# Down projection with the activations as the stationary operand, and the sampled tokens in plain single precision on four column groups

## The reference

```
x = x + concat([oa, ob]) @ w_out
h = rms_norm(x, norm_ffn)                               # (288, 2048)
y = x + (silu(h @ w_gate) * (h @ w_up)) @ w_down        # w_gate, w_up: 2048 x 5632, w_down: 5632 x 2048
```

## Time and profile before

| | us |
|---|---|
| median of 3 runs | 1440.21 (1435.78 to 1446.68) |
| the profiled execution, its own time | 1442.6 |
| its span, first to last instruction | 1440.8 |
| PE busy | 1423.8 (99%) |
| DVE busy | 760.1 (53%) |
| ACT busy | 539.8 (37%) |

### The profile page before, as it was taken

One profiled execution on the slowest core, in us unless ns is written; L12 is line 12 of the kernel. 1 busy time (PEld: TensorE's weight loads), 2 busy tenths in 40 slices (PEclk: granted clock), 3 DMA queues, 4 the chain that ended last, 5 costly groups with the idle time before them and its releaser, 6 DMA issues.

```text
span 1440.8 us, 23855 instructions
## 1 busy us (share of the span) xinstructions
PE 1423.8 (99%) x10403; PEld 1375.2 (95%) x10403; DVE 760.1 (53%) x937; ACT 539.8 (37%) x650; POOL 116.0 (8%) x134
## 2 busy tenths in 40 slices
PE   6999999999999999999999999999999999999998
PEld 4999999998989899999999999999999999999998
DVE  4435655565543465744555464555555554545454
ACT  7336975321113433433233333333332333333322
POOL 2010421111220006100000000000000000000000
PEclk9999999997789999999999999999999999999999
DMA  8695555524455454655656556555555565655552
GB/s 235 176 324 136 160 142 148 135 73 115 117 155 187 133 163 147 169 155 174 172 151 176 154 168 173 161 165 173 150 176 158 164 172 152 174 166 162 170 168 74
DMA packets 320193, 231.32 MB, mean 161 GB/s; under 512 B 4838, under 2 KB 291823, under 8 KB 319514
## 3 DMA queue, kind: packets, MB, share of 16 engines
q1 hardware_dynamic: 314000, 206.06, 49.7%
q0 software_dynamic: 5856, 23.59, 5.4%
q10 hardware_dynamic: 234, 0.16, 0.0%
HBM read 219.99 MB, written 14.97 MB: 163 GB/s over the span
## 4 chain that ended last, share of the span: by engine, by line
PE 98%; DMA 1%; ACT 0%; DVE 0%; issue 0%; SPq 0%; ACTq 0%; DVEq 0%
PE acc L1450 29%; PE acc L1454 29%; PE acc L1451 28%; PE mx L1615 3%; PE mx L1687 1%; PE mx L1675 1%; PE mx L1405 1%; DMA reg_qkf<-in_x_prompt_dram 1%; PE acc L1470 1%; PE acc L1464 1%; PE mx L1544 0%; PE mx L1516 0%; PE mx L1476 0%; PE mx L1896 0%; PE mx L1590 0%; PE mx L1531 0%
## 5 line engine op out<-in xcount | busy, mean ns | idle before, releaser
L1450 PE MATMUL acc<-act_h,wh 128*128 128x288 f32 x2208 | 605.4, 303 | 0.0
L1451 PE MATMUL acc<-act_l,wh 128*128 128x288 f32 x2208 | 601.7, 298 | 0.0
L962 DVE TENSOR_TENSOR wl<-raw,wh 128x2048 fp32r<-128x2048 f32 x192 | 440.6, 2295 | 57.4 <-PE acc L1454 52.4
L609 ACT ACTIVATE wh<-raw 128x2048 fp32r<-128x2048 f32 x192 | 366.5, 1910 | 237.0 <-PE acc L1454 227.9
L1450 PEld LDWEIGHTS acc<-act_h,wh 128*128 128x128 f32 x2208 | 422.9, 192 | 5.1 <-issue 4.3
L1451 PEld LDWEIGHTS acc<-act_l,wh 128*128 128x128 f32 x2208 | 421.4, 191 | 0.0
L1454 PE MATMUL acc<-act_h,wl 128*128 128x288 f32 x2208 | 327.0, 301 | 0.0
L1454 PEld LDWEIGHTS acc<-act_h,wl 128*128 128x128 f32 x2208 | 306.3, 192 | 4.9 <-issue 4.7
L1450 PE MATMUL acc<-mix_h,wh 128*128 128x288 f32 x832 | 228.6, 299 | 0.0
L1451 PE MATMUL acc<-mix_l,wh 128*128 128x288 f32 x832 | 227.8, 295 | 0.0
L1450 PEld LDWEIGHTS acc<-mix_h,wh 128*128 128x128 f32 x832 | 157.1, 189 | 2.4 <-issue 2.3
(11 more groups left out here) (251 smaller groups left out, 765.4 us busy)
## 6 DMA issues: line engine op xcount, KB each, us to landing
raw<-in_w_in_dram SPq DMA_DIRECT2D x44, 1024.0 KB, 5.9
raw<-in_w_gate_dram SPq DMA_DIRECT2D x44, 1024.0 KB, 5.6
raw<-in_w_up_dram SPq DMA_DIRECT2D x44, 1024.0 KB, 5.6
raw<-in_w_down_dram SPq DMA_DIRECT2D x44, 1024.0 KB, 5.1
raw<-in_w_out_dram SPq DMA_DIRECT2D x16, 1024.0 KB, 5.4
reg_x<-in_state_hgrn_dram POOLq DMA_DIRECT2D x8, 512.0 KB, 5.0
out_dram<-reg_x POOLq DMA_DIRECT2D x8, 512.0 KB, 4.4
bias_rows<-bias_line POOLq DMA_DIRECT2D x1, 3072.0 KB, 15.4
```

Source lines behind the costliest of these rows:

```text
L609: nc.scalar.activation(wh[:, s % WH, :], raw[:, s % RAW, :], ACT.Copy).then_inc(high_done, 1)
L962: nc.vector.tensor_tensor(wl[:, s % WL, :], raw[:, s % RAW, :], wh[:, s % WH, :].bitcast(F32), ALU.subtract).then_inc(low_done, 1)
L1450: mm(out, w_h[:, i, cols], a_hi[:, place(i), :], start=(i == 0), stop=False)
L1451: mm(out, w_h[:, i, cols], a_lo[:, place(i), :], start=False, stop=False)
```

## The change

The down projection swaps its operands. For each slab there are now three pieces (`piece`), each with 512 output columns in one of the four banks `mx`, and added by DVE into `xtok` (token by token):
- the 32 sampled tokens: four matmuls in plain single precision, stationary 128 x 32 inner activations (`inner_s`), moving the raw slab of 512 columns per k-tile. The four k-tiles go to four groups of 32 output partitions, so their sums stay apart until the very end, when `sample_sums` adds them with four more matmuls (stationary `token_sum`);
- the 128 first and the 128 last prompt tokens: 4 k-tiles x 3 = 12 matmuls each, the activations stationary (128 x 128), the weights moving 512 columns.

The residual must therefore be token by token before the first addition: the four `y_group`s move from the last chunk to the first, ahead of units 4 to 7 of gate_up(0), with their copies on ACT and DVE. POOL clears the tile of the sampled tokens before. A load into a `raw` buffer also waits for the sampled matmuls that read it. Gate and up matmuls stay as they are.

```diff
@@ SP, load
                 if s >= RAW:
                     sp.wait_ge(low_done, s - RAW + 1)
+                if s - RAW in down_of:
+                    sp.wait_ge(samp_done, down_of[s - RAW] + 1)
@@ SP, end
-            for q in range(4):
-                cols = slice(512 * q, 512 * q + 512)
-                sp.wait_ge(yt_copied_a, 2 * q + 2)
-                sp.wait_ge(yt_copied_v, q + 1)
+            for i in range(DN):
+                cols = slice(512 * i, 512 * i + 512)
                 for j in range(2):
+                    sp.wait_ge(down_added, piece(NCH - 1, i, 1 + j) + 1)
                     sp.dma_start(y_prompt[...], xtok[:, j, cols]).then_inc(y_out, 16)
-                sp.dma_start(y_sample[...], xtok[0:TS, 2, cols]).then_inc(y_out, 16)
+                    if i == DN - 1 and j == 0:
+                        sp.wait_ge(ys_copied, 1)
+                        for n in range(4):
+                            sp.dma_start(y_sample[...], y_s[TS * n:TS * n + TS, :]).then_inc(y_out, 16)
@@ ACT, gate_up
-                        nc.scalar.activation(mix_h[:, FC * (c % 2) + t, :], tmp[:, 4 + t % 2, :], ACT.Copy)\
+                        nc.scalar.activation(mix_h[:, FC * (c % 2) + t, 0:TP], tmp[:, 4 + t % 2, 0:TP], ACT.Copy)
+                        nc.scalar.activation(inner_s[:, c % 2, t, :], tmp[:, 4 + t % 2, TP:T], ACT.Copy)\
                             .then_inc(innerh_done, 1)
                     ahead(gu_slab(c) + i, units_ffn(c, i, False))
+                    if c == 0 and i >= 4:
+                        y_copies(i - 4)
@@ DVE, gate_up
                     ahead(gu_slab(c) + i, units_ffn(c, i, False))
+                    if c == 0 and i >= 4:
+                        y_copy(i - 4)
@@ DVE, down
-                    for n in range(4):
-                        m = 4 * i + n
...
-                        nc.vector.tensor_tensor(xT[:, m, :], acc[n][:, 0:T], xT[:, m, :], ALU.add)\
+                    for n in range(3):
+                        u = piece(c, i, n)
...
+                        j = (2, 0, 1)[n]
+                        nc.vector.tensor_tensor(xtok[:, j, cols], mx[:, u % 4, :], xtok[:, j, cols], ALU.add)\
                             .then_inc(down_added, 1)
@@ PE, gate_up
+                    if c == 0 and i >= 4:
+                        y_group(i - 4)
                     s = gu_slab(c) + i
                     pe.wait_ge(high_done, s + 1)
@@ PE, y_group
-                pe.wait_ge(down_added, 16 * (NCH - 1) + 4 * q + 4)
-                if q:
+                if q == 0:
+                    pe.wait_ge(x_added, 32)
+                    pe.wait_ge(rstd2_done, 1)
+                else:
                     pe.wait_ge(yt_copied_a, 2 * q)
                     pe.wait_ge(yt_copied_v, q)
@@ PE, new
+            def sample_tokens(c, i):
+                w = raw[:, (dn_slab(c) + i) % RAW, :].rearrange("p (k c) -> p k c", k=FC)
+                for k in range(FC):
+                    ins = mm(mx[TS * k:TS * k + TS, piece(c, i, 0) % 4, :], inner_s[:, c % 2, k, :], w[:, k, :],
+                             start=True, stop=True)
+                ins.then_inc(samp_done, 1)
+            def prompt_tokens(c, i, j):
...
+                for k in range(FC):
+                    mm(out, mix_h[:, half + k, tokens], w_h[:, k, :], start=(k == 0), stop=False)
+                    mm(out, mix_l[:, half + k, tokens], w_h[:, k, :], start=False, stop=False)
+                if j == 0:
+                    pe.wait_ge(low_done, s + 1)
+                for k in range(FC):
+                    ins = mm(out, mix_h[:, half + k, tokens], w_l[:, k, :], start=False, stop=(k == FC - 1))
+                ins.then_inc(unit_done, 1)
@@ PE, down
+                    for n in range(3):
+                        if piece(c, i, n) >= 4:
+                            pe.wait_ge(down_added, piece(c, i, n) - 3)
+                        if n == 0:
+                            sample_tokens(c, i)
                         else:
+                            prompt_tokens(c, i, n - 1)
+                        if c == NCH - 1 and i == DN - 1 and n == 1:
+                            sample_sums()
```

More of the change, by code:

```diff
@@ L405, in dn_slab, with piece @@
             return S_FFN + 8 * min(c + 2, NCH) + 4 * c
+        down_of = {dn_slab(c) + i: 4 * c + i for c in range(NCH) for i in range(DN)}
+        def piece(c, i, n):
+            return 12 * c + 3 * i + n
         def ffn_walk(gate_up, down):
@@ L591, in _ @@
                     nc.gpsimd.tensor_tensor(tmp[:, 0, :], tmp[:, 0, :], tmp[:, 1, :], ALU.add).then_inc(sq2_done, 1)
+            pool.wait_ge(hl_done, AH)
+            nc.gpsimd.memset(xtok[:, 2, :], 0.0).then_inc(y_zero, 1)
             pool.wait_ge(outs, 16 * n_outs[0])
@@ L943, in _ @@
             ffn_walk(gate_up, down)
-            for q in range(4):
-                y_copies(q)
+            act.wait_ge(ys_done, 1)
+            nc.scalar.activation(y_s, mx[:, 0, :], ACT.Copy).then_inc(ys_copied, 1)
         @block.vector
@@ L1898, in y_group @@
                 ins.then_inc(yt_done, 1)
+            def sample_tokens(c, i):
[5 more added lines that the diff above has]
+            def prompt_tokens(c, i, j):
+                s = dn_slab(c) + i
+                w_h = wh[:, s % WH, :].rearrange("p (k c) -> p k c", k=FC)
+                w_l = wl[:, s % WL, :].rearrange("p (k c) -> p k c", k=FC)
+                out = mx[:, piece(c, i, 1 + j) % 4, :]
+                half = FC * (c % 2)
+                tokens = slice(P * j, P * j + P)
+                for k in range(FC):
[6 more added lines that the diff above has]
+                ins.then_inc(unit_done, 1)
@@ L1900, in down, with sample_sums @@
+            def sample_sums():
+                pe.wait_ge(down_added, piece(NCH - 1, DN - 1, 0) + 1)
+                for n in range(4):
+                    ins = mm(mx[TS * n:TS * n + TS, 0, :], token_sum, xtok[:, 2, 512 * n:512 * n + 512],
+                             start=True, stop=True)
+                ins.then_inc(ys_done, 1)
             def down(c):
-                half = FC * (c % 2)
                 pe.wait_ge(innerl_done, FC * c + FC)
+                if c == 0:
+                    pe.wait_ge(yt_copied_a, 8)
+                    pe.wait_ge(yt_copied_v, 4)
+                    pe.wait_ge(sum_made, 1)
@@ L1903, in down @@
                 for i in range(DN):
-                    s = dn_slab(c) + i
-                    pe.wait_ge(high_done, s + 1)
-                    for n in range(4):
-                        m = 4 * i + n
-                        if m >= 4:
-                            pe.wait_ge(down_added, 16 * c + m - 3)
-                        elif c == NCH - 1:
-                            pe.wait_ge(down_added, 16 * (c - 1) + 12 + n + 1)
-                        else:
-                            pe.wait_ge(inner_done if n % 2 else gate_scaled, (c + 1) * FC + 2 + n // 2 + 1)
-                        passes(n, dn_slab(c) + i, FC, slice(P * n, P * n + P), mix_h[:, half:half + FC, :],
-                               mix_l[:, half:half + FC, :],
-                               lambda: pe.wait_ge(low_done, s + 1) if n == 0 else None)
-                        if n == 1 and i and c == NCH - 1:
-                            y_group(i - 1)
+                    pe.wait_ge(high_done, dn_slab(c) + i + 1)
```

44 lines of the change are left out of this document (27 added, 17 removed).

## The result

| | before | after |
|---|---|---|
| median of the runs, us | 1442.97 (4 runs, 1435.78 to 1446.68) | 1476.41 (4 runs, 1472.51 to 1480.77) |
| ratio, 95% interval | | 1.0239 [1.0186, 1.0292] |
| span of the profiled execution, us | 1440.8 | 1475.5 |
| its own time, us | 1442.6 | 1477.45 |

The change costs 33 us; 1458 were forecast, with 1474 as the upper end. The time before has one more run here than the prediction had.

The account below looks back on a forecast made before the run. PE was taken to bound the kernel, busy 1423.8 of 1440.8 us. Terms -1.8 + 15.2 + 6 - 2.0 = +17.4 on 1442.6 gave 1460, or 1458 us at the runs' median; range 1447 to 1474.

Parts of the forecast that it names:

- The 512-column matmul: Down projection: price of one wide matmul, taken as 0.215 us, so 24 per slab take 5.16 us.
- a floor from the weight load: Down projection: the extra 0.013 us at 288 columns comes from the weight load and is hidden at 512, giving 0.215 us.
- toll per matmul: Down projection: alternative reading, each wide matmul pays the 0.013 us too, 0.228 us; bound +12 us.
- the term -1.8: Down projection: new slab 6.36 us against 6.40, over 44 slabs -1.8 us.
- a dearer wide matmul: Down projection rival: toll or slower stream, 0.228 us giving 1471 us or 0.237 giving 1481; chance 14%.
- A slab off by over 0.2 us: Down projection: sign that the prediction is wrong, a slab differing from 6.36 us by that much, 9 us in all.
- The sampled tokens: Down projection: four matmuls on four overlapping column groups, two rounds of 0.43 us plus switching, 1.20 us a slab.
- What moves at nothing: Down projection and its surroundings: DVE additions, ACT's extra copy, weight loads, POOL's memset stay covered, at no cost.
- The moved transposes: First feed-forward chunk: PE waits 4.6 us on copies three times, 13.9 us, plus 1.3 for the fourth group; +15.2 us.
- The clock: First feed-forward chunk: granted clock falls after each of three gaps, 1.5 to 3 us a time, 2 taken; +6 us.
- The rival in which it does not fall: First feed-forward chunk: gaps stay but the clock holds, +11.4 us or 1452 us; chance 15%.
- The end: After the last matmul's start: 3.8 us remain instead of 7.0, sampled sums cost 1.2; -2.0 us.

Follow-up runs that it names:

- e10_low: Changed kernel with PE held before the first down slab by three POOL memsets, so the first wide matmuls run at the low clock; 1490.56 us.
- e12_pair: Changed kernel with e1_early's edit and the sampled bursts of two slabs put together ahead of both slabs' wide matmuls; 1453.06 us, ratio 1.0095 to the kernel before.
- e9_serial: Changed kernel with a slab's four sampled matmuls on one column group instead of four; 1588.06 us.
- e5_m32: Changed kernel with 32 instead of 128 stationary tokens in each prompt matmul of the down projection; 1466.8 us.
- e1_early: Changed kernel with the ACT and DVE copies of the transposes moved ahead of serving the unit beside them; 1458.04 us, ratio 1.0112 to the kernel before.
- e8_plain: Changed kernel with the third (low) product of the prompt tokens in plain single precision on the same operands; 1698.41 us.
- e11_nosamp: Changed kernel without the sampled tokens in the down projection, one more wide matmul per slab in their place; 1430.85 us.
- e4_384: Changed kernel with every prompt piece of the down projection split into matmuls of 384 and 128 columns; 1533.15 us.
- e2_fill: Changed kernel with 32 unused 288-column matmuls ahead of each of the three waits for transpose copies; 1474.7 us, ratio 1.0237.

## Why the prediction was wrong

**The 512-column matmul: the step that failed.** The prediction read 0.1333 us for 288 columns against 0.120 at 2.4 per ns, asked whether the 0.013 was "a floor or a toll", and took "a floor from the weight load, which a longer stream hides", so 0.215. It is neither a floor (256 columns take 0.119) nor a toll per matmul (0.228), but nearly all grows with the columns: 0.2333. Twenty-four times 0.018 is 0.44 us a slab, 19.3 us over 44, and that is the miss: the term -1.8 became +17.2. The evidence used to choose was the low clock, where the matmul has no toll. That row speaks against a fixed share but not against a limit on how fast columns arrive, which the low clock never reaches; e10_low shows that 512 columns look just as innocent there. The plain-precision rows priced another type. Halving their 0.43 us holds in time (a plain record takes 0.86 us at the low clock, a quick-type matmul with as many columns 0.427), but the quick type does not keep that pace at the higher clock. The rival "a dearer wide matmul" (14%, 1471 to 1481) named what came, a price that grows with the columns, and holds the result. The bounds had it, but the range stopped at 1474 and left its dearer half out. A slab off by over 0.2 us was the prediction's own sign of being wrong, and it is off by 0.43.

**The sampled tokens: right in size.** Forecast 1.20, measured 1.19, out of two rounds of 0.43 and a price of 0.33 for going in and out. In the kernel before a slab with one qk square takes 7.18 us instead of 6.40. The square's first record ends 0.43 us after its start and both 0.67 (from 97.08), so a record is 0.24 and two are 0.48, and 0.30 is left for going in and out. The 0.03 that the term has more no run shows as such; what the runs showed in its place is 0.33 in the slabs and 0.32 in e12_pair. The overlap of four groups, inferred from the earlier trace rows, is shown by e9_serial, and that the price is one per burst by e12_pair. What it is paid for no run shows; the step from 128 to 32 output columns is not all of it, since in e5_m32, which has no such step, 0.24 of it stay.

**What moves at nothing: right.** PE's idle column is 0.0 in all groups of the down projection; the additions, the loads and the extra copy stay covered.

**The moved transposes: right.** Three waits of 4.3 to 4.7 us on DVE's copies were named, 4.41, 4.47 and 4.41 came, and the 13.9 for them measured 13.8. e1_early shows that the order of the copies is the cause. The late weight load behind the transposes is there too: in the kernel before it starts at 1430.65, 0.02 us ahead of its matmul at 1430.67, where the next ones start 0.13 ahead (1430.76 for the matmul at 1430.89), and the matmul's record lasts 0.38 instead of 0.29.

**The clock: right in kind, a little dear for this execution.** It fell behind each wait for 3.4 us, the shortest stretch known from the earlier trace rows, and took 1.4 to 1.5 a time, not 2. That is the low end of the forecast's 1.5 to 3; and it lay mostly over the transposes (2.79 us instead of 1.50), not "over dense work". Term +6, measured +4.4. In e5_m32, e8_plain and e11_nosamp two of the three low stretches were 6.8 us long and the three groups cost some 2 us more, so +6 describes those executions as well as +4.4 does this one. The rival in which it does not fall is refuted.

**The end: right.** 3.8 us from the last matmul's start and 1.2 for the sums, together -2.0 as forecast.

So the sum was +17.4 and came to +34.7: 19.0 too little for the slabs, 1.6 too much for the clock. Two errors of the forecast's form stand beside it: 44 slabs multiply one unseen price, so that price deserved the widest range of all terms; and with both bounds above the chosen value and none below, 14% for everything above it was too little.

## What to carry to other kernels

Before a stream is made of fewer and wider matmuls, count its columns, not its instructions: here 48 x 288 = 13824 columns a slab became 24 x 512 = 12288 of the quick type (5.60 us instead of 6.40). The sampled tokens' four groups run side by side, but in two rounds of 0.43 us. With the price of going in and out they add 1.19 us, so that the new slab took longer than the old (6.79 us against 6.40). A price for an unseen size is to be scaled from the same number type at the same clock, by two sizes if there are any, and where one price is multiplied by 44 the range must hold its dearest reading. A copy that another engine waits for belongs ahead of the wait for the next unit, not behind it: that alone was 18 us.

## What the runs showed of the hardware

- At the higher clock a matmul of the quick type starts every 0.119, 0.1333, 0.1755, 0.2333 us with 256, 288, 384, 512 columns, a line of 2.24 columns per ns. At the lower clock it has no such loss (0.24 for 288, 0.427 for 512, both 1.2 columns per ns).
- A plain single-precision matmul of 512 columns leaves two records. One takes 0.429 us at the higher clock (e8_plain) and 0.86 at the lower (e10_low), there twice the quick type's 0.427.
- Matmuls of the quick type with 128 columns and a full weight load each came every 0.111 us (e4_384), above the line.
- Entering a burst of single-precision matmuls with 32 output columns and leaving it costs 0.32 to 0.33 us a time in a stream of the quick type, with 8 records inside as with 16; where the stream has 32 output columns too, some 0.09 of that go away and 0.24 stay. A change to single precision at 128 output columns costs nothing that can be seen (e8_plain).
- Waits of 4.41 to 4.47 us without a matmul were followed by the lower clock each time, for 3.4 us in some executions (the changed kernel, e4_384) and for 6.8 in others (the first two waits of e5_m32, e8_plain, e11_nosamp); with matmuls in the gap, however useless, the clock stayed at 1.00 (e2_fill).
